# Eight pairs of heads in a recurrent block: six state steps, first blocks on three engines, one direction's streams on GpSimd, turnings between the steps, gates made once

## The chip, the cores and the metric

One Trainium2 chip, one of its cores. The metric is the device time of one execution in microseconds; everything is float32. Engines: TensorE (PE, with its weight loads PEld), VectorE (DVE), ScalarE (ACT), GpSimd (POOL), SyncE (SP), and the DMA queues.

## What is computed

Two blocks of a model run one after the other over 256 tokens of width 2048. The change touches only the second block, and in it the part called RWKV: 16 heads of 64 channels, each with two recurrences (forward and backward in time), first over 256 context tokens and then, from the state reached, over the 256 tokens of the sequence:

```python
def wkv_scan(r, w, k, v, kk, a, s0, reverse):
    def step(s, inp):
        r_t, w_t, k_t, v_t, kk_t, a_t = inp
        sa = jnp.einsum('bhij,bhj->bhi', s, -kk_t)
        s = (s * w_t[:, :, None, :] + sa[..., None] * (kk_t * a_t)[:, :, None, :]
             + v_t[..., None] * k_t[:, :, None, :])
        return s, jnp.einsum('bhij,bhj->bhi', s, r_t)
...
    y = yf + yb
    mu = jnp.mean(y, axis=-1, keepdims=True)
    var = jnp.mean(jnp.square(y - mu), axis=-1, keepdims=True)
    y = ((y - mu) * lax.rsqrt(var + GN_EPS) * ln_w + ln_b)
    y = y + jnp.sum(r * (kf + kb) * r_k, axis=-1, keepdims=True) * v
    g = jax.nn.sigmoid(gd) @ g_up
    return y.reshape(b, l, D_RWKV) * g, (sf, sb)
```

Only the outputs of the sequence are used. Its result goes, with two small mixers, through `w_out`; a feed-forward part and a norm follow.

## The kernel before, in words

The program is written out engine by engine (`sp_program`, `pool_program`, `pe_program`, `act_program`, `dve_program`); an engine does its instructions in the order of the text, and waits on semaphores by name: `need(name, j, k)` waits until pair j has counted k on that name, and `o.do(ins, S(name))` or `done(mm, name)` counts. `o.settle()` lets an engine wait for its own last instruction.

The heads are done in pairs, j = 0 to 7 (`NP2 = 8`); 128 partitions hold the two heads. Each pair has two directions, d = 0 and 1, and eight chunks of 64 tokens (`CH`): four of context, four of sequence. The programs of this stage are `pairs_pe` (from L1745), `pairs_act` (L2092), `pairs_dve` (L2423) and the loop in `pool_program` (L1474). The steps of one pair are:

- *Decays and keys.* `decays` (PE L1760, L1761) multiplies the small decay and rate weights, which GpSimd loads pair by pair (`ups`, L1460); `sigmoids` (ACT), `sums` (DVE: a scan and a subtraction), `key_sums`, `key_roots`, `key_inverse`, `key_spread`, `key_norms`, `keys` (DVE L2458), `key_mixes` and `exponentials` (ACT, three for each direction; all of pairs_act goes by the helper's line L2097).
- *Streams* (DVE L2461 to L2487, eight instructions of 128x512 or 128x256 for each direction): products of decays, keys and rates, all in SBUF. Direction 1 reads the keys backwards (`seq`). Direction 0 of the next pair is done after level 5; direction 1 in six parts between the state steps.
- *Turnings* (`by_token`, PE L1788, L1789): four for each pair, each turns two of the streams into banks 2 and 3; `token_copies` (ACT) copies both out before the next turning.
- *Scores* (PE): AX (L1801, L1803) and BR (L1813, L1817), 64x64 products of each cell, into banks 0 to 7.
- *First blocks* (`starts`, DVE L2492 to L2508): masks AX into `aT` and `xm` and makes the first level's mask `mT`; masks BR into `bT` and `rpk`; and, from the turned products (`turned_starts`, PE L1829), `xmT`.
- *Levels 1 to 5* of a triangular inversion by doubling: P (PE L1843) of `mT` and `xm`; `products` (ACT) copies; Y (PE L1856, L1858); DVE subtracts Y from `xm` and `xmT` (L2517, L2518). GpSimd makes the masks of levels 2 to 5 (L1472). Between the levels PE does head means, the gate and variances of pair j-1 and sums, decays and norms of pair j+1. DVE does, of pair j-1, `centred` (before level 1's subtractions), `variances` (before level 2's), and `normed` (before level 3's), which also multiplies by the gate in bank 7 and counts `pair_end`.
- *Right sides and solution*: `solved` (PE BV L1881, U L1888), `right_sides` (ACT: two copies within SBUF, two out of PSUM), `solutions` (ACT).
- *Steps* (PE L1900 to L1930; DVE L2548 to L2558): Z, the step matrices and the read-outs, for d = 0, then d = 1. The step matrix of a chunk is the identity minus a product.
- *States* (PE L1939, DVE `stt` of 128x64 by the helper L2436): m = 0 to 7, both directions. State 0 is zero. Streams of direction 1 and turnings 0 and 1 of the next pair stand between them, turning 2 behind them, then `outputs` (PE L1949, DVE L2572 to L2578), then turning 3 and the next scores.

The gate weights (`g_up`, 128x256 for each pair) are loaded by GpSimd in front of the masks of level 4, after `pair_end` (L1463), and the gate is computed in each pair (PE L1869). The last pair has no next one; after its level 3, DVE makes the sums of the mixed rows of pairs 0 to 6 (`mix_sums`, L2332 to L2337) for the product with `w_out`.

```python
        for j in range(NP2):
            masks(j, 2)
            masks(j, 3)
            need("pair_end", j, 0)
            gate_up(j * P, lambda ins: ...)
            masks(j, 4)
            masks(j, 5)
```

## Time and profile before

| | |
|---|---|
| median of 3 runs | 3397.76 us (3395.79 to 3398.54) |
| the profiled execution | 3396.16 us, its span 3394.3 us |
| busy, share of the span | PE 92%, PEld 82%, DVE 47%, ACT 16%, POOL 33% |
| preparation of the pairs | 1809 to 1843 us |
| the eight pairs | 1843 to 2397 us |
| PE, P of the levels (L1843) | 2560 instructions, 226 ns each |
| GpSimd, 128x512 masks (L1472) | 64 instructions, 1342 ns each |
| q8, the queue that brings instructions | 253 packets, 4.15 MB |

Times are counted from the start of the span. "Idle before" is how long an engine stood still ahead of an instruction, and the arrow names what ended it; "issue" means that nothing that the profile shows was late. Matmul records overlap, so that busy PE is not PE at its peak. PEclk is the clock that TensorE was granted, 1.00 being 2.4 GHz and 0.50 1.2 GHz.

### The profile page before, as it was taken

The page shows a single profiled execution, that of the slowest core. Times are in us where ns is not written, and L with a number is a line of the kernel's source. Part 1 is how long each engine was busy: PE and PEld are TensorE (multiplying, and loading weights), DVE is VectorE, ACT ScalarE, POOL GpSimd, SP SyncE. Part 2 cuts the span into 40 slices and gives each one's busy share as a digit, 9 for nine tenths or more (in the row PEclk, how much of TensorE's full clock was granted, in tenths as well). Part 3 has the DMA queues.
Part 4 walks back from the last instruction along what each step waited for, and adds up shares of the span by engine and source line. Part 5 has one row for each costly group of instructions (what it writes and reads, how often), then busy time and mean ns, then how long its engine had stood idle before and what let it go on. Part 6 is the DMA issues. An engine that isn't in the chain of part 4 may idle for free.

```text
span 3394.3 us, 69586 instructions
## 1 busy us (share of the span) xinstructions
PE 3112.3 (92%) x32190; PEld 2794.7 (82%) x32190; DVE 1596.5 (47%) x2384; ACT 544.6 (16%) x1022; POOL 1109.8 (33%) x621
## 2 busy tenths in 40 slices
PE   5998999998999999999896888777999999999998
PEld 4877887877878888687895777666889999999998
DVE  4745275455437610587814666666334442113111
ACT  1012112021210111100003443343010000000001
POOL 1000000000000010243671211112447797778774
PEclk8998999998999999999997999999899999999999
DMA  7955387765335643477640000000445654444443
GB/s 281 405 224 198 120 316 286 306 246 205 107 145 216 231 177 139 172 274 288 250 150 11 10 7 7 7 7 6 162 149 224 227 221 170 161 167 162 162 166 109
DMA packets 56035, 583.10 MB, mean 172 GB/s; under 512 B 7314, under 2 KB 9680, under 8 KB 10816
## 3 DMA queue, kind: packets, MB, share of 16 engines
q1 hardware_dynamic: 37808, 465.06, 36.7%
q0 software_dynamic: 17936, 113.59, 8.8%
q8 instruction: 253, 4.15, 0.5%
q14 instruction: 38, 0.31, 0.0%
HBM read 576.52 MB, written 2.10 MB: 170 GB/s over the span
## 4 chain that ended last, share of the span: by engine, by line
PE 70%; DVE 13%; DMA 9%; issue 3%; ACT 3%; POOL 2%; SPq 0%; ACTq 0%; DVEq 0%; POOLq 0%
PE PS L1675 24%; PE PS L374 14%; PE PS L672 7%; PE PS L1628 5%; DMA ring<-in_w_vec_dram 5%; DMA ring<-in_w_second_dram 2%; DVE ring L2244 2%; PE PS L417 2%; PE PS L1843 1%; DMA ring<-in_w_start_dram 1%; PE PS L371 1%; PE PS L1856 1%; PE PS L1692 1%; PE PS L1611 1%; PE PS L1888 1%
## 5 line engine op out<-in xcount | busy, mean ns | idle before, releaser
L374 PE MATMUL PS<-H,ring 128*128 128x256 f32 x2944 | 669.4, 386 | 7.0 <-ACT H L702 7.0
L374 PEld LDWEIGHTS PS<-H,ring 128*128 128x128 f32 x2944 | 562.6, 193 | 95.0 <-issue 17.6
L1675 PE MATMUL PS<-H,ring 128*128 128x128 f32 x3424 | 404.5, 276 | 1.5 <-DMA ring<-in_w_second_dram 1.5
L1675 PEld LDWEIGHTS PS<-H,ring 128*128 128x128 f32 x3424 | 394.7, 193 | 2.4 <-DMA ring<-in_w_second_dram 1.9
L2351 DVE TENSOR_TENSOR W<-W,PS 128x256 f32<-128x256 f32 x58 | 24.4, 421 | 679.8 <-ACT W L2001 679.7
L327 POOL DMA_DIRECT2D ring<-in_w_vec_dram x75 | 39.7, 530 | 923.9 <-DVE ring L888 785.7
L1675 PE MATMUL PS<-H,W 128*128 128x128 f32 x2624 | 316.6, 276 | 8.4 <-POOL W L1504 7.2
L1675 PEld LDWEIGHTS PS<-H,W 128*128 128x128 f32 x2624 | 305.0, 193 | 9.7 <-POOL W L1504 8.0
L1499 POOL TENSOR_TENSOR W<-ring 128x1024 f32<-128x1024 f32 (+1 forms) x74 | 179.7, 2429 | 265.7 <-PE PS L1675 149.2
L672 PE MATMUL PS<-H,ring 128*128 128x256 f32 x1024 | 223.5, 379 | 2.9 <-DVE H L1174 2.9
L672 PEld LDWEIGHTS PS<-H,ring 128*128 128x128 f32 x1024 | 194.2, 190 | 29.9 <-issue 3.7
L1472 POOL TENSOR_TENSOR ring<-ring,W 128x512 f32<-128x512 f32 x64 | 84.9, 1342 | 367.1 <-PE PS L1843 366.7
L888 DVE SCALAR_TENSOR_TENSOR ring<-ring,H 128x2048 f32<-128x2048 f32 x75 | 171.1, 2287 | 29.3 <-DMA ring<-in_w_vec_dram 28.6
L1504 POOL TENSOR_TENSOR W<-ring,W 128x1024 f32<-128x1024 f32 (+1 forms) x74 | 182.4, 2465 | 5.8
L1502 POOL TENSOR_TENSOR W<-W,ring 128x1024 f32<-128x1024 f32 (+1 forms) x74 | 181.6, 2455 | 0.0
L1501 POOL TENSOR_TENSOR ring<-ring 128x1024 f32<-128x1024 f32 (+1 forms) x74 | 177.4, 2398 | 5.8
L1628 PE MATMUL PS<-H,ring 128*128 128x128 f32 (+1 forms) x992 | 142.5, 306 | 9.8 <-DMA ring<-in_w_second_dram 4.9
L1628 PEld LDWEIGHTS PS<-H,ring 128*128 128x128 f32 x992 | 134.4, 199 | 16.5 <-issue 5.7
L2244 DVE SCALAR_TENSOR_TENSOR ring<-ring,W 128x2048 f32<-128x2048 f32 x48 | 127.2, 2666 | 38.5 <-DMA ring<-in_w_vec_dram 38.0
L2001 ACT ACTIVATE W<-PS 128x128 f32<-128x128 f32 (+2 forms) x61 | 18.6, 307 | 786.1 <-PE PS L1675 777.3
L1675 PE MATMUL PS<-Pj,ring 128*128 128x128 f32 x1184 | 139.8, 275 | 3.3 <-DVE H L2337 3.3
L1675 PEld LDWEIGHTS PS<-Pj,ring 128*128 128x128 f32 x1184 | 135.9, 192 | 3.5 <-issue 3.5
(500 smaller groups left out, 4990.5 us busy)
## 6 DMA issues: line engine op xcount, KB each, us to landing
ring<-in_w_second_dram SPq DMA_DIRECT2D x97, 2048.0 KB, 8.1
ring<-in_w_first_dram SPq DMA_DIRECT2D x68, 2048.0 KB, 8.3
ring<-in_w_vec_dram POOLq DMA_DIRECT2D x75, 1024.0 KB, 7.8
ring<-in_w_vec_dram SPq DMA_DIRECT2D x48, 1024.0 KB, 5.1
ring<-in_w_start_dram SPq DMA_DIRECT2D x16, 2048.0 KB, 15.7
H<-in_w_vec_dram POOLq DMA_DIRECT2D x21, 1024.0 KB, 8.1
Pj<-in_w_aside_dram SPq DMA_DIRECT2D x8, 2048.0 KB, 11.2
ring<-in_w_second_dram SPq DMA_DIRECT2D x9, 1536.0 KB, 6.6
```

The costliest lines, as they stand in the source:

```text
L374: mm = pe.matmul(PS[:, t % 2, half * T:(half + 1) * T], ring[:, t % 2, k, half * P:(half + 1) * P], hT[:, k, :], start=(k == 0), stop=(k = ...
L417: mm = pe.matmul(PS[:, t, half * T:(half + 1) * T], left, right, start=(k == 0 and half == 0), stop=(k == KC - 1), skip_group_check=True)
L672: mm = pe.matmul(PS[:, 4 + 2 * (n % 2) + half, 0:T], ring[:, t % 2, k, half * P:(half + 1) * P], hT[:, k, :], start=(k == 0), stop=(k == K ...
L888: return v.scalar_tensor_tensor(out, a, s, b, op0, op1, **kw)
L1472: S("p_mask").inc(pool.tensor_tensor(mT[d], aT[d], Ci(f"c_join{lev}").unsqueeze(1).to_broadcast([P, 8, CH]), ALU.mult))
L1499: sums.inc(pool.tensor_tensor(s_[:, 0], quarter(q, 2, nk), quarter(q, 3, nk), ALU.add))
L1501: sums.inc(pool.tensor_tensor(quarter(q, 2, nk), quarter(q, 0, nk), quarter(q, 2, nk), ALU.subtract))
L1502: sums.inc(pool.tensor_tensor(s_[:, 1], s_[:, 0], quarter(q, 0, nk), ALU.subtract))
L1504: sums.inc(pool.tensor_tensor(s_[:, 2], quarter(q, 1, nk), s_[:, 1], ALU.subtract))
L1628: mm = pe.matmul(in_regions(n % 2, wide, r), w[:, k * P:(k + 1) * P], at(m, k), start=(k == 0 and r // per not in opened), stop=(k == 7), ...
L1675: mm = pe.matmul(regions(bank2, r), w[:, k * P:(k + 1) * P], m[:, k, :], start=(first and k == 0 and r // 4 not in opened), stop=(last and ...
L2244: v.scalar_tensor_tensor(w, w, 1.0, crow2[:, 0, :], ALU.mult, ALU.mult, accum_out=mod2[:, i - 64, 0:1]).then_inc(vec_done.sem, 1)
```

## The change

- *State steps*: m = 1 to 6. Step 1 takes its state from `Z[d][:, 0]`; states 0 and 8 are no longer made (no memset).
- *First blocks*: DVE keeps `aT`, `xm`, `xmT`; GpSimd makes level 1's mask and masks `bT` and `rpk` in place (`below`); ACT copies BR out of PSUM, and does the right sides' SBUF copies there too. `xmT` of both directions is masked before the first subtraction.
- *Streams*: direction 1 goes to GpSimd (`stream_back`), in one piece, behind the masks of the pair before.
- *Turnings*: each waits bank by bank, and all four stand between the state steps 1 to 4.
- *Gates*: all weights come in one load of 1 MB on SyncE's queue, one tile before the last input tile; all eight gates are computed in the preparation and copied by ACT into `mix`.
- Pair j-1: `centred` after level 1's subtractions, variances between the two directions of level 2 on PE and DVE, the reciprocal after level 3, the rest after level 4. The mixed rows' sums go after level 4.
- Steps: the read-out subtraction before the step matrices, and a wait of PE moved behind G. `bonus` (one instruction instead of two) goes between the states. ACT does `solutions` before the second direction's exponentials.

```diff
@@ sp_program
+            if q == NIN2 - 2:
+                sp.wait_ge(vec_done.sem, vec_done.at(NL, VEC0[3] - VEC0[2]))
+                S("gate_loaded").inc(sp.dma_start(gup, A["g_up_2"][0].rearrange("(d p) c -> p d c", d=2)), 16)
@@ pool_program
         def masks(j, lev):
             for d in range(2):
-                need("p_P", j, count(lev - 1, d))
...
+                if lev == 1:
+                    need("p_aT", j, d + 1)
+                else:
+                    need("p_P", j, count(lev - 1, d))
...
+        def below(j, d):
+            need("p_BRr", j, d + 1)
+            pool.tensor_tensor(bT[d], bT[d], each8(Ci("c_supper")), ALU.mult)
+            pool.tensor_tensor(rpk[d], rpk[d], each8(Ci("c_upper")), ALU.mult)
+        def stream_back(j):
+            need("p_tm", j, 2)
+            need("p_kk", j, 1)
+            S("p_akr").inc(pool.tensor_tensor(AA[1], AA[1], seq(KK, 1), ALU.mult))
+            S("p_akr").inc(pool.tensor_tensor(TMP[1], TMP[1], seq(key(j), 1), ALU.mult))
+            need("p_bonus", j, 1)
+            need("p_akr", j, 2)
+            S("p_akr").inc(pool.tensor_tensor(BN(j).unsqueeze(1), BN(j).unsqueeze(1), TMP[1][:, 1:2, ::-1], ALU.add))
+            need("p_exp", j, 2)
+            pool.tensor_tensor(EV[1], EV[1], seq(KK, 1), ALU.mult)
+            pool.tensor_tensor(AA[1], AA[1], EN[1], ALU.mult)
+            pool.tensor_tensor(RT(j, 1).unsqueeze(1), EP[1][:, 1:2, :], seq(rec(j), 1), ALU.mult)
+            S("p_akr").inc(pool.tensor_copy(ends(j, 1), flat(EP[1])[:, CH - 1::CH]))
+            need("p_akr", j, 4)
+            S("p_strr").inc(pool.tensor_tensor(EN[1], TMP[1], EN[1], ALU.mult))
+        stream_back(0)
         for j in range(NP2):
+            masks(j, 1)
             masks(j, 2)
+            below(j, 0)
             masks(j, 3)
-            need("pair_end", j, 0)
-            gate_up(...)
+            below(j, 1)
             masks(j, 4)
             masks(j, 5)
...
+            if j < NP2 - 1:
+                stream_back(j + 1)
@@ pairs_pe
+        def gates(n):
+            for j in (2 * n, 2 * n + 1):
+                for k in range(2):
+                    mm = pe.matmul(PS[:, gate_banks[n], (j % 2) * T:(j % 2 + 1) * T], gup[:, k, j * P:(j + 1) * P], GD[:, k, :], ...)
+            done(mm, "mix_gate")
         def by_token(j, r):
...
+            for w in range(2):
+                if r:
+                    need("p_tokc", j, taken(r - 1, w))
+                elif j:
+                    need("p_step", j - 1, 2)
+                for n in range(4):
+                    mm = pe.transpose(PS[:, 2 + w, t], src[w][:, t], ident)
+                done(mm, "p_tokT")
@@ level: the variances between the directions of Y
+                if d and between:
+                    between()
@@ head_means
-            for k in range(2):
-                mm = pe.matmul(PS[:, 7, 0:T], gup[:, k * P:(k + 1) * P], GD[:, k, :], start=(k == 0), stop=(k == 1))
@@ the pair on TensorE
             steps(j)
-            for m in range(8):
+            for m in range(1, 7):
                 state(j, m)
-                if after and m in (1, 3):
-                    by_token(j + 1, m // 2)
-            if after:
-                by_token(j + 1, 2)
+                if after and m < 5:
+                    by_token(j + 1, m - 1)
             outputs(j)
             if after:
-                by_token(j + 1, 3)
                 scores(j + 1)
@@ pairs_act
+        def below(j):
+            need("p_tokc", j, 8)
+            for d in range(2):
+                f("p_act", kbv[d]..., Ktok_[d]..., ACT.Copy)
+            for d in range(2):
+                need("p_BR", j, d + 1)
+                f("p_BRr", br[d], PS[:, 4 + 2 * d:6 + 2 * d, :].rearrange(...), ACT.Copy)
...
             right_sides(j)
+            solutions(j)
             if after:
                 exponentials(j + 1, 1)
-            solutions(j)
-            if after:
                 for r in range(4):
                     token_copies(j + 1, r)
+                below(j + 1)
@@ pairs_dve
+            need("p_xt", j, 1)
+            for e in range(2):
+                o.do(v.tensor_tensor(per_head(xmT[e]), heads(2, e * T), each(Ci("c_join0")), ALU.mult))
+            o.settle()
+            for e in range(2):
+                o.do(stt(xmT[e], xmT[e], -1.0, all8(Ci("c_ident")), ALU.mult, ALU.add), S("p_x0"))
@@ the pair on VectorE
             starts(j)
+            level(j, 1)
             if before:
                 centred(j - 1)
-            level(j, 1)
-            if before:
-                variances(j - 1)
-            level(j, 2)
+            level(j, 2, (lambda: variances(j - 1)) if before else None)
             if after:
                 key_squares(j + 1)
-            if before:
-                normed(j - 1)
             level(j, 3)
             if after:
                 key_inverse(j + 1)
+            if before:
+                inverse(j - 1)
+            level(j, 4)
+            if before:
+                normed(j - 1)
...
-            for m in range(8):
+            for m in range(1, 7):
                 state(j, m)
-                if after and m < 6:
-                    stream(j + 1, 1, m)
+                if m == 1:
+                    bonus(j)
             outputs(j)
```

## Rows read from the trace of the kernel before

**Rows 1.** The page's part 4: the chain that ended last, by engine.
```profile
PE 70%; DVE 13%; DMA 9%; issue 3%; ACT 3%; POOL 2%; SPq 0%; ACTq 0%; DVEq 0%; POOLq 0%
```

**Rows 2.** Busy time by stretch: start:end, length, each engine, PEclk, DMA share, GB/s.
```profile
1809.00:1843.00 34.00, 18.56 (x64) 11.58 (x68) 12.78 (x25) 16.95 (x27) 3.17 (x5) 0.55 0.07 21
...
2047.00:2117.00 70.00, 57.24 (x1794) 50.48 (x1794) 46.30 (x96) 28.48 (x52) 12.42 (x11) 0.95 0.03 8
```

**Rows 3.** Waits of TensorE, 2047 to 2117: us in total, times, longest.
```profile
PE PS L1856 <- DVE ring L2436: 2.4, 1, 2.4
PE PS L1843 <- DVE ring L2517: 2.1, 2, 1.7
...
PE PS L1843 <- issue: 1.3, 1, 1.3
PE PS L1926 <- DVE Pj L2558: 1.3, 1, 1.3
...
PE PS L1888 <- ACT ring L2097: 0.8, 1, 0.8
```

**Rows 4.** Timeline, pair 3: start, us, engine, line, operation, idle before.
```profile
2055.93 1.58 POOL L1472 TENSOR_TENSOR ring<-ring,W 128x512 f32<-128x512 f32 x1 [0.59 <-PE PS L1843]
2057.02 1.04 DVE L2436 SCALAR_TENSOR_TENSOR ring<-ring,W 128x512 f32<-128x512 f32 x1
...
2063.10 1.03 PE L1869 MATMUL PS<-Pj,W 128*128 128x256 f32 x4
2065.79 0.41 PE L1843 MATMUL PS<-ring 64*64 64x64 f32 x7 [1.66 <-DVE ring L2517]
...
2078.34 2.50 POOL L1472 TENSOR_TENSOR ring<-ring,W 128x512 f32<-128x512 f32 x2
2078.38 0.68 DVE L2517 TENSOR_TENSOR ring<-ring,PS 128x512 f32<-128x512 f32 x1
```

**Rows 5.** Busy time by short stretch, columns as in rows 2.
```profile
2058.20:2062.10 3.90, 3.77 (x128) 3.68 (x129) 1.06 (x2) 0.02 (x1) 0.00 (x0) 0.56 0.01 4
2081.90:2084.10 2.20, 2.20 (x137) 2.13 (x133) 0.94 (x2) 0.60 (x1) 1.86 (x2) 1.00 0.03 7
1813.60:1817.40 3.80, 3.75 (x4) 1.18 (x4) 0.11 (x1) 1.17 (x1) 0.00 (x0) 0.50 0.00 0
```

**Rows 6.** Groups by shape, 1840 to 2400: busy us, mean ns, idle before.
```profile
L1843 PE MATMUL PS<-ring 64*64 64x64 f32 x2560 | 94.3, 226 | 25.1 <-DVE ring L2517 18.0 <-issue 3.3 <-POOL ring L1472 3.0
...
L1472 POOL TENSOR_TENSOR ring<-ring,W 128x512 f32<-128x512 f32 x64 | 84.9, 1342 | 367.1 <-PE PS L1843 366.7
...
L2535 DVE RECIPROCAL Pj<-Pj 128x256 f32<-128x256 f32 x7 | 12.2, 1743 | 0.0
...
L2097 ACT ACTIVATE ring<-ring 128x512 f32<-128x512 f32 x16 | 9.9, 617 | 2.7 <-PE PS L1881 2.7
...
L2487 DVE TENSOR_TENSOR W<-W 128x512 f32<-128x512 f32 x14 | 9.6, 687 | 0.2
```

**Rows 7.** Timeline of TensorE in the state steps, pair 3 and the last pair.
```profile
2105.55 0.33 PE L1939 MATMUL PS<-Pj,ring 64*64 64x64 f32 x4 [0.26 <-DVE Pj L2436]
...
2107.02 0.33 PE L1939 MATMUL PS<-Pj,ring 64*64 64x64 f32 x4
...
2112.54 0.33 PE L1788 MATMUL PS<-con,W 128*128 128x128 f32 x1
...
2391.00 0.33 PE L1939 MATMUL PS<-Pj,ring 64*64 64x64 f32 x4 [0.20 <-DVE Pj L2436]
...
2391.72 0.33 PE L1939 MATMUL PS<-Pj,ring 64*64 64x64 f32 x4 [0.20 <-DVE Pj L2436]
```

**Rows 8.** The chain that ended last, first two turnings of pair 0: start, us.
```profile
1831.27 0.47 PE PS L1788
...
1834.51 0.45 PE PS L1788
```

**Rows 9.** The same chain behind the last pair's outputs.
```profile
2396.99 8.10 DMA ring<-in_w_second_dram
```

197 lines of the change are left out of this document (91 added, 106 removed).

## The prediction

> **What bounds the kernel now.** I read the page's chain first: TensorE holds 70% of it and VectorE 13% [rows 1]. The edit touches only the eight pairs of heads of the second block, so I cut that stage into stretches that run from one pair's first score matmul to the next one's. There are nine: 34 us of preparation, and then 66, 68, 70, 70, 72, 69, 71 and 68 us. In such a pair of 70 us TensorE is busy 57.2 us, VectorE 46.3, ScalarE 28.5 and GpSimd 12.4 [rows 2]. So nothing is full. TensorE stands still for some 12 us a pair, and its work itself is stretched where the granted clock is low. The pair is one chain that goes from engine to engine and back.
>
> Who ends these idle times is in the waits of that pair [rows 3]: VectorE before the first level's second products (2.4), VectorE before the second level (most of 2.1), VectorE in the eight state steps and before the outputs' first part (1.3), ScalarE before the solving products (0.8), and "issue", where no engine is late (1.3 is the longest). Whoever shortens VectorE's list at these places shortens the pair.
>
> The timeline shows two things more. The wait of 1.66 us before the second level follows the head means and four matmul records of the gate; in it VectorE does the centring of the pair before ahead of this level's subtractions [rows 4]. And the 128 matmuls of the first level's second products take 3.8 us at a clock of 0.56, while 137 of the same kind take 2.2 us at 1.00 [rows 5]; they come right after the idle 2.4 us. The 1.66 us of idleness was followed by full clock.
>
> **The lock.** In the same group a VectorE instruction that reads two SBUF operands takes 1.04 us where its mates take 0.69: it ends 0.55 us after GpSimd's instruction ends, and that one has grown to 1.58, where two of them take 2.50 [rows 4, 6]. Beside it a VectorE instruction with one operand in PSUM takes its usual 0.68 in the middle of GpSimd's work [rows 4]. So instructions of the first sort and GpSimd's take turns. The Trainium skill (SBUF — State Buffer, "Who interferes with whom") says the same of two SBUF inputs and calls it an exclusive lock; by that rule, moving one direction's streams to GpSimd buys no parallel time where VectorE runs the other direction's streams, all of whose inputs lie in SBUF.
>
> **The change, part by part**, for one of the six pairs that have a neighbour on both sides.
>
> (1) *First blocks.* VectorE loses six of its sixteen instructions there (two level masks, four masks of the second half), 0.69 us each [rows 6]. But what TensorE waits for lies at the end: after the turned products VectorE did product, subtraction, product, subtraction, and both directions had to be ready. Now two products come first and direction 0 is released after one subtraction: one instruction less, 0.6 to 1.0 us. Against it GpSimd's first and second masks and its two masks of "below" now fall beside the VectorE subtractions with two SBUF inputs, each good for up to one GpSimd instruction, 1.3 us [rows 6]. Taken: -0.5, between +0.7 and -1.6.
>
> (2) *Between first and second level.* The four gate records (0.9 us) go, since gates are made once, and the centring moves behind the subtractions, so that the 1.66 us go as well [rows 4]: 2.6 us. ScalarE's squares wait for the centring and stand before its copies of level 2, but means end about when those copies are wanted. The rest is clock: the gap before the first level's second products shrinks by part (1); if they run at full clock that is 1.8 us [rows 5]. I take half of it, as the new gap is about as long as the 1.66 us. Taken: -3.5, between -2.0 and -4.5.
>
> (3) *Levels 2 to 4.* The normalisation (a reciprocal of 1.74 us [rows 6] and three more instructions, 3.2 us together) stood before level 3's subtractions and goes to two later places, where VectorE has time until the next products end; the variance matmul is put between the two directions; GpSimd no longer waits for the pair's end to load the gate's weights before masking level 4. TensorE's waits for these are the remainder of the 2.1 [rows 3] and GpSimd's 3.0 us over eight pairs [rows 6]. Taken: -1.1 with the variance, between -0.3 and -2.0. Late next would be the next pair's first sums on VectorE, which have the decay matmuls of TensorE as cover.
>
> (4) *Right sides.* ScalarE's two copies within SBUF (0.62 us each [rows 6]) leave the place before the solving products; one of them stood before direction 0. Of the 0.8 us waited [rows 3] 0.5 goes. Taken: -0.5, between -0.3 and -0.6. At their new place, "below", they stand behind the token copies and before the copies of the BR products; the cover is the score matmuls and level 1's first products.
>
> (5) *Steps.* The subtraction of the read-outs comes before the step matrices on VectorE (0.75 us), a memset goes, and TensorE's wait for the first Z moves behind the second G: of the 1.3 us waited [rows 3] and 0.3 before, 1.4 goes. Against it, VectorE's stream for the next pair now collides with the first two GpSimd instructions of the other direction (2.7 us), just ahead of these steps. There was about 1.5 us of slack and part (4) eats 0.5: some 0.6 comes back. Taken: -0.8, between 0 and -1.9.
>
> (6) *States and turnings.* A step with a turning between it and the next takes 1.47 us (2105.55 to 2107.02), one without 0.72 in the last pair, where VectorE has nothing else [rows 7]. Now: first step 0.7, seven steps with two turnings from 2105.55 to 2112.54, 7.0, and two more turnings of 1.1 behind: 9.9. New: four steps with a turning, 5.9, and two without, 0.8 each: 7.5. VectorE also sheds the eight stream instructions between the steps. Taken: -2.3, between -1.5 and -2.6.
> What covers it: the third turning needs GpSimd's stream. Its two first instructions start with the keys, together with VectorE's own stream; the second half (EV, AA, RT, ends, EN: three of 1.34, one of half that, 4.7 us) starts after the exponentials, which ScalarE now does behind the solution copies. By the timeline that puts its end some 2.4 us before the third turning is due. If that cover is gone, each us over 2.4 is a us on the pair.
>
> Sum for such a pair: -0.5 -3.5 -1.1 -0.5 -0.8 -2.3 = **-8.7 us**, six times: -52. Pair 0 has no (2) and (3): -4. The last pair has no turnings; its states lose two steps of 0.72, it saves 2.5 us on levels 3 and 4, because the normalisation no longer stands ahead of level 3 and the sums of the mixed rows go one level later, and gives 0.5 back there: -9 with (1), (2) and (5).
>
> *Preparation.* Now the turnings start at 1831.27 and follow each other every 3.24 us, since one waits for both copies of the other [rows 8]. New: two banks alternate, so that a turning costs about 1.6 us: 3 x 1.6 = 5 us less. But GpSimd's stream ends there near 1836 if nothing else changes, which gives some 2 of them back, and the four groups of gates, sixteen matmuls, go in: eight into TensorE's idle time before the keys, and eight behind the key norms. They cost 3.5 us for each eight at full clock, 7 at half. Against that the decay matmuls run at 0.50 now, 3.8 us [rows 5], and with the gates ahead of them TensorE is not idle before. Bounds: nothing gained at half clock; -9 at full. Taken: -5.
> The gate's weights (1 MB) move from GpSimd's queue to SyncE's, ahead of the last input tile; a load of 2 MB takes 8.1 us [rows 9], and TensorE takes longer than that for an input tile, which is the cover. Cost nothing; with the cover gone, half a load, 4 us once. *Tail*: SyncE's loads start with the last output and TensorE waits 8.1 us for them [rows 9]; this is unchanged and only comes earlier. What follows is TensorE at over 90% and moves as a whole.
>
> Sum: -52 -4 -9 -5 = -70 us. The profiled execution took 3396.16 us (span 3394.3 and 1.9 around it), 1.6 under the median 3397.76 of the three runs; so 3396 - 70 = **3326 us**.
>
> **Rivals.**
> *A, the clock comes back* (chance 0.20). With TensorE busy in more of the pair, first products and turnings run at 1.00 throughout. Then (1) and (2) reach their ends (-1.3, -4.5), (5) -1.4: about -11.5 a pair, -95 in all, 3301. For: the half-speed stretches all follow idle times that shrink. Against: the new gap before the first level's second products is no shorter than some that were followed by it.
> *B, the lock takes a share* (0.15). Each of GpSimd's 24 instructions a pair (8 now, beside its DMAs) meets VectorE's two-operand ones more often than I placed them: (1) +0.5, (2) -2.6, (5) 0, (6) -1.5, so -5 a pair, -40 in all: 3356. For: the collision in rows 4 cost each of the two 0.3 to 0.4 us. Against: most of GpSimd's masks fall beside VectorE instructions that read PSUM.
> *C, slower* (0.04): GpSimd's stream is late for the third turning. No row has GpSimd reading backwards (step -1), and five of its ten instructions do. It decides when the stream ends 2.4 + 8.7 = 11 us later than I place it. At five times the 1.34 us, these take 6.7 each: 16.7 us before the exponentials' part and 12.7 for it, 29.4 from the keys on, where I place the end at 11.6; that is 18 us, or 15 behind the slack: +6.7 a pair, +40 for the six, +11 for pair 0, -9 for the last, +10 in the preparation: 3448. VectorE's backward reads cost nothing more in its rows, so this is unlikely.
> *D, TensorE's "issue" waits fill up* (0.08): they are 3 us a pair, in dense stretches of small matmuls. If the supply of instructions is the limit there, a denser pair meets more of them, and half of the gain goes: 3361.
> *E, no change* (0.03): the six terms are all waits that something just behind also ends.
> The forecast itself has 0.50.
>
> **Numbers.** Faster: 0.50 + 0.20 + 0.15 + 0.08 = 0.93; same 0.03; slower 0.04 (0.2%, 7 us, is what a measurement of this kernel can tell from no change). The forecast's own ends, half way to the terms' ends, are 3308 and 3348; to hold eight in ten the range goes to A's value and past B's: 3298 to 3362.
>
> **What would show it.** Pairs of some 61 us instead of 70; no wait of TensorE for VectorE's subtraction before the second level; first level's second products at 1.00 in some pairs; states and turnings in 7.5 us with the outputs right behind; GpSimd busy some 25 us a pair; VectorE's streams longer than 0.69 us each beside GpSimd's. Wrong it would be if the turnings waited for GpSimd, if the level masks came late, or if the preparation grew by the gates.

## The result, and the profile of the changed kernel

The changed kernel takes **3319.44 us** in the median of four runs (3315.47 to 3320.62), the kernel before 3398.15 us in the same session (3395.79 to 3400.12): a ratio of 0.977, with an interval of 0.975 to 0.978. The forecast was 3326 us with a range from 3298 to 3362. The profiled execution took 3319.18 us (span 3317.4), against 3396.16 for the one that the sum was made on: -77.0 us where -70 was expected.

The chain of the page, by engine, in the place of [rows 1]: TensorE keeps its share.

```profile
PE 70%; DVE 14%; DMA 9%; issue 3%; POOL 2%; ACT 1%; SPq 0%; ACTq 0%; DVEq 0%; POOLq 0%
```

Busy time by stretch, columns as in [rows 2]: the preparation, pair 0, pair 3 and the last pair, cut at the first score matmul of each pair.

```profile
1805.87:1836.60 30.73, 19.04 (x90) 13.93 (x88) 14.03 (x20) 20.37 (x32) 13.26 (x13) 0.89 0.07 23
1836.60:1898.06 61.46, 51.33 (x1764) 45.69 (x1765) 38.67 (x67) 31.89 (x56) 28.80 (x24) 0.97 0.03 7
2018.94:2078.18 59.24, 51.52 (x1783) 45.30 (x1780) 43.34 (x76) 30.74 (x54) 28.84 (x24) 1.00 0.03 7
2258.35:2316.30 57.95, 46.04 (x1731) 41.99 (x1727) 37.27 (x66) 13.56 (x25) 18.55 (x14) 0.91 0.02 4
```

Pair 3 went from 70.3 to 59.2 us. TensorE is busy 5.7 us less in it and idle 5 us less; GpSimd went from 12.4 to 28.8 us. The waits of TensorE in this pair, in the place of [rows 3]:

```profile
PE PS L1906 <- DVE ring L2496: 2.6, 2, 2.0
PE PS L1972 <- DVE Pj L2599: 1.0, 1, 1.0
PE PS L1947 <- issue: 1.0, 1, 1.0
PE PS L1891 <- issue: 0.9, 1, 0.9
...
PE PS L1934 <- ACT ring L2145: 0.3, 1, 0.3
```

The first row, the wait before the first level's second products (L1906), is as long as before (2.4 then). The wait for VectorE's subtraction before the second level (2.1 us at the line of the levels' first products before) is gone; the issue wait of 0.9 at that line (L1891) stands in the first level, at 2025.8. The solving products (L1934) wait 0.3 for ScalarE, not 0.8.

The same place in the timeline, in the place of [rows 4]: VectorE's two subtractions with both operands in SBUF, and GpSimd beside them.

```profile
2028.20 1.27 POOL L1482 TENSOR_TENSOR ring<-ring,W 128x512 f32<-128x512 f32 x1 [0.60 <-PE PS L1891]
2028.56 3.14 DVE L2496 SCALAR_TENSOR_TENSOR ring<-ring,W 128x512 f32<-128x512 f32 x2
2029.42 1.73 POOL L1487 TENSOR_TENSOR ring<-ring,W 128x512 f32<-128x512 f32 x1
2031.10 1.73 POOL L1488 TENSOR_TENSOR ring<-ring,W 128x512 f32<-128x512 f32 x1
```

Two subtractions take 3.14 us, and each of GpSimd's masks of BR beside them 1.73 where the mask of level 2 (L1482) takes 1.27. The mask of level 2 had started first, before the subtraction. The same happens in the streams of the next pair: GpSimd's first two instructions take 1.70 and 1.72, and VectorE's second 1.76 instead of 0.69.

```profile
2059.94 0.69 DVE L2525 TENSOR_TENSOR W<-W,Pj 128x512 f32<-128x512 f32 x1
2060.06 1.70 POOL L1494 TENSOR_TENSOR W<-W,Pj 128x512 f32<-128x512 f32 x1 [6.18 <-DVE Pj L2518]
2060.55 1.76 DVE L2526 TENSOR_TENSOR W<-W,Pj 128x512 f32<-128x512 f32 x1
2061.72 1.72 POOL L1495 TENSOR_TENSOR W<-W,Pj 128x512 f32<-128x512 f32 x1
...
2066.66 1.27 POOL L1500 TENSOR_TENSOR W<-W,Pj 128x512 f32<-128x512 f32 x1 [1.89 <-ACT W L2145]
2070.07 1.27 POOL L1505 TENSOR_TENSOR W<-W 128x512 f32<-128x512 f32 x1
```

L1500 reads one operand backwards and still takes 1.27. The stream ends at 2071.34; the third turning, which needs it, starts at 2073.49. The steps, in the place of [rows 7]:

```profile
2071.61 0.33 PE L1986 MATMUL PS<-Pj,ring 64*64 64x64 f32 x4
...
2073.08 0.33 PE L1986 MATMUL PS<-Pj,ring 64*64 64x64 f32 x4
...
2076.61 0.33 PE L1986 MATMUL PS<-Pj,ring 64*64 64x64 f32 x4 [0.27 <-DVE Pj L2496]
...
2077.42 0.68 PE L1996 MATMUL PS<-Pj 64*64 64x64 f32 x16 [0.29 <-DVE Pj L2496]
```

A step with a turning takes 1.47 us as before, and from the first step (2070.21) to the outputs it is 7.2 us.

**Phases.** To compare kernels I took from the trace when the first record of each kind of product starts, and averaged over the six middle pairs. The columns: from the first scores to the first level's second products; from there to the first products of level 2; levels 2 to 4; level 5 and the right sides up to the solving products; from these to the first step; from the first step to the next pair's scores; the sum; then pair 0, the last pair, and the preparation, from the end of the transform's products to the first scores. Each kernel's phases come from its one profiled execution. The time before this stage, in which nothing was edited in any run, lasted 1798.6 to 1808.7 us in the profiles of the changed kernel and its variants, so that a difference of some us between two totals need not lie in the pairs.

| kernel | scores, level 1 | to level 2 | levels 2-4 | level 5, right sides | solving, steps' products | states, turnings, outputs | pair | pair 0 | last | prep. |
|---|---|---|---|---|---|---|---|---|---|---|
| before | 11.6 | 7.3 | 21.2 | 8.4 | 10.3 | 11.3 | 70.0 | 66.2 | 67.7 | 35.0 |
| changed | 11.5 | 4.4 | 18.0 | 7.9 | 10.2 | 8.0 | 60.0 | 61.5 | 57.8 | 30.7 |
| forecast of the difference | -0.5 | -3.5 | -1.1 | -0.5 | -0.8 | -2.3 | -8.7 | -4 | -9 | -5 |
| measured difference | -0.1 | -2.9 | -3.2 | -0.5 | -0.1 | -3.2 | -10.0 | -4.7 | -9.9 | -4.3 |

What TensorE does in these phases, us a pair over the same six pairs (waits over 0.15 us, from the trace):

| | scores, level 1 | to level 2 | levels 2-4 | level 5, right sides | solving, steps' products | states, turnings, outputs | pair |
|---|---|---|---|---|---|---|---|
| waits for an engine, before | 2.4 | 1.7 | 0.5 | 1.1 | 1.4 | 2.1 | 9.2 |
| the same, changed | 2.1 | 0.4 | 0.0 | 0.6 | 1.2 | 0.6 | 4.8 |
| issue waits, before | 1.3 | 0.4 | 2.0 | 0.0 | 0.4 | 0.0 | 4.1 |
| the same, changed | 1.9 | 0.0 | 0.4 | 0.0 | 0.6 | 0.0 | 3.0 |
| busy, before | 7.8 | 5.3 | 18.6 | 7.3 | 8.5 | 9.2 | 56.6 |
| the same, changed | 7.6 | 4.0 | 17.6 | 7.3 | 8.3 | 7.4 | 52.2 |

So the 10.0 us are 4.4 of waits for other engines, 4.4 of TensorE's own busy time and 1.1 of issue waits. In the busy time there is the work that was taken away, and up to 1.4 us of clock: the granted clock over these pairs rose from 0.968 to 0.986.

### The profile page after: what moved, and what is told of

It reads as the page before. It is cut to its first block, busy times and chain, and to the rows that moved or that the text cites. A ratio compares the mean times of both kernels' runs of the same rounds, so it can differ in the third digit from the quotient of the medians.

```text
span 3317.4 us, 69293 instructions
## 1 busy us (share of the span) xinstructions
PE 3078.1 (93%) x32062; PEld 2768.7 (83%) x32062; DVE 1578.4 (48%) x2216; ACT 564.4 (17%) x1042; POOL 1234.7 (37%) x725
## 3 DMA queue, kind: packets, MB, share of 16 engines
q8 instruction: 252, 4.13, 0.5%
## 4 chain that ended last, share of the span: by engine, by line
PE 70%; DVE 14%; DMA 9%; issue 3%; POOL 2%; ACT 1%; SPq 0%; ACTq 0%; DVEq 0%; POOLq 0%
PE PS L1712 23%; PE PS L374 15%; PE PS L672 7%; PE PS L1665 5%; DMA ring<-in_w_vec_dram 4%; DMA ring<-in_w_second_dram 2%; PE PS L1891 2%; DVE ring L2304 2%; PE PS L417 2%; DMA ring<-in_w_start_dram 1%; PE PS L371 1%; PE PS L1908 1%; PE PS L1906 1%; PE PS L1837 1%; PE PS L1729 1%
## 5 line engine op out<-in xcount | busy, mean ns | idle before, releaser
L374 PEld LDWEIGHTS PS<-H,ring 128*128 128x128 f32 x2944 | 562.1, 193 | 94.9 <-issue 17.6
L672 PEld LDWEIGHTS PS<-H,ring 128*128 128x128 f32 x1024 | 194.2, 190 | 29.9 <-issue 3.7
L1482 POOL TENSOR_TENSOR ring<-ring,W 128x512 f32<-128x512 f32 x80 | 101.0, 1276 | 159.2 <-DVE ring L2543 82.5
L2049 ACT ACTIVATE W<-PS 128x128 f32<-128x128 f32 (+2 forms) x61 | 18.6, 307 | 789.5 <-PE PS L1712 780.5
L2145 ACT ACTIVATE ring<-PS 128x512 f32<-128x512 f32 (+2 forms) x232 | 121.6, 568 | 162.1 <-PE PS L1891 56.6
## 6 DMA issues: line engine op xcount, KB each, us to landing
Pj<-in_w_aside_dram SPq DMA_DIRECT2D x8, 2048.0 KB, 11.3
```

The lines of the kernel that those rows point to most:

```text
L374: mm = pe.matmul(PS[:, t % 2, half * T:(half + 1) * T], ring[:, t % 2, k, half * P:(half + 1) * P], hT[:, k, :], start=(k == 0), stop=(k = ...
L672: mm = pe.matmul(PS[:, 4 + 2 * (n % 2) + half, 0:T], ring[:, t % 2, k, half * P:(half + 1) * P], hT[:, k, :], start=(k == 0), stop=(k == K ...
L1482: S("p_mask").inc(pool.tensor_tensor(mT[d], aT[d], each8(Ci(f"c_join{lev}")), ALU.mult))
L2145: S(name).inc(act.activation(out_, in_, fn, **kw))
```

## The experiments

**Centring first.** The one order on VectorE that the change turned round is turned back.

```diff
-            level(j, 1)
             if before:
                 centred(j - 1)
+            level(j, 1)
             level(j, 2, (lambda: variances(j - 1)) if before else None)
```

> The changed kernel with one thing undone: VectorE does the centring of the pair before ahead of level 1's subtractions again, not behind them. TensorE's order stays. By step (2) of the prediction this wait is worth 1.66 us in each of the seven pairs that have one before them, and some clock may go with it: 1.7 to 2.6 us a pair, 12 to 18 in all, 3331 to 3337 us, and TensorE's idle time of about 1.7 us for VectorE behind the head means is back. Rival (GpSimd's masks for level 2 end there just behind, so that the order on VectorE is worth little): under 0.5 us a pair, 3319 to 3323. Clock theory (the order matters only because the idle time costs clock): the phase grows by no more than 1 us where the granted clock stays, and by 2 or more where it falls.

Measured: 3344.40 us, ratio 0.984 (0.982 to 0.987), 25 us above the changed kernel where 12 to 18 were expected. A pair takes 63.2 us instead of 60.0. The phase to level 2 grows by 1.8 us, and levels 2 to 4 by 1.2. The waits of TensorE over the six middle pairs of this run:

```profile
PE PS L1906 <- DVE ring L2496: 14.9, 11, 2.1
PE PS L1891 <- DVE ring L2559: 10.0, 6, 1.7
PE PS L1891 <- issue: 7.4, 6, 1.5
```

The second row is the wait of 1.66 us that was foretold: 10.0 over six, and it fills the 1.8 us. The rest is no wait for VectorE: all issue waits of these pairs sum to 22.1 us instead of 17.8, 0.7 a pair, and TensorE is busy 0.6 us more a pair at a clock of 0.98 instead of 0.99 (316.8 against 313.0 over six). TensorE's program is the same to the last instruction, so the issue waits are worth a look of their own.

**Turnings late.**

```diff
-                if after and m < 5:
-                    by_token(j + 1, m - 1)
+                if after and m in (2, 4):
+                    by_token(j + 1, m // 2 - 1)
+            if after:
+                by_token(j + 1, 2)
             outputs(j)
             if after:
+                by_token(j + 1, 3)
```

> The changed kernel with the four turnings back at their old places relative to the steps: the first two behind the second and fourth of the six steps, the third behind the last step, the fourth behind the outputs. Six steps are kept. By step (6): two steps with a turning (1.47 each), four without (0.72 to 0.8) and two turnings alone (1.1 each) make 8.1 us where the changed kernel has 7.3 to 7.5: +0.6 to 0.8 us in each of seven pairs, +4 to +6, 3323 to 3325. Rival (GpSimd's stream is just in time for the third turning, and what the denser order wins is given to waits): -0.5 to +0.3 a pair, 3316 to 3321.

Measured: 3325.17 us, ratio 0.978 (0.977 to 0.980); a pair takes 61.3 us. Steps, turnings and outputs went from 8.0 to 8.7 us: +0.7, as priced. The other 0.6 lies in the phase to level 2 at a lower clock (0.97 over these pairs against 0.99).

**Eight steps.** Steps 1 and 6 are done twice.

```diff
-            for m in range(1, 7):
-                state(j, m)
-                if after and m < 5:
-                    by_token(j + 1, m - 1)
+            for i, m in enumerate((1, 1, 2, 3, 4, 5, 6, 6)):
+                state(j, m, i + 1)
+                if after and i < 4:
+                    by_token(j + 1, i)
```

> The changed kernel with eight state steps a pair again: the first and the sixth are done twice, with the same values, and the four turnings stay behind the first four. By step (6) each extra step without a turning costs 0.72 to 0.8 us: +1.5 us a pair over eight pairs, +12, 3331 us. Rival (the two steps were hidden: TensorE has the next pair's turnings to do and VectorE's chain is not what ends last): +0 to +3, 3319 to 3322.

Measured: 3344.05 us, ratio 0.983 (0.980 to 0.986), again 25 us above, where 12 were expected; the four runs lie far apart (3326.62 to 3350.35). The phase of the steps grew from 8.0 to 9.7, +1.7 for two steps: the price of step (6) holds. But the pair grew by 3.3, and in it the issue waits by 1.3 (25.4 us over six pairs against 17.8); TensorE's lower clock, 0.97, is in the rest.

**Masks held.** GpSimd waits for the end of VectorE's subtractions.

```diff
             masks(j, 2)
+            need("p_x0", j, 2)
             below(j, 0)
```

> The changed kernel with one wait more on GpSimd: its two masks of direction 0 of what lies below (of BR) wait until VectorE's last subtraction of the first blocks is over. Nothing is moved on another engine. Lock theory (VectorE's instruction with two SBUF operands and GpSimd's take turns, and the subtraction of 3.14 us with the record at 2028.56 is 1.3 us of work and the rest GpSimd's masks): the longest of these subtractions falls to 2 us or less, TensorE's waits for it (2 x 1.3 us) lose 1.2 to 2 us a pair, 10 to 14 us in all: 3305 to 3310. Rival (a subtraction with these operands is simply slow there, or GpSimd's level 2 mask alone does it): under 0.5 us a pair, 3316 to 3321. Against both: if GpSimd's masks of level 3 come late because of the hold, up to 1 us a pair the other way.

Measured: 3322.23 us, ratio 0.977 (0.975 to 0.980), where 3305 to 3310 was expected. The profiled execution, 3313.53 us, was the fastest of four (the slowest 3327.75), so that the total shows no gain and the phases have to. Pair 3 of that run:

```profile
2030.52 1.27 POOL L1482 TENSOR_TENSOR ring<-ring,W 128x512 f32<-128x512 f32 x1 [0.60 <-PE PS L1892]
2030.88 2.06 DVE L2497 SCALAR_TENSOR_TENSOR ring<-ring,W 128x512 f32<-128x512 f32 x2
2033.02 1.27 POOL L1487 TENSOR_TENSOR ring<-ring,W 128x512 f32<-128x512 f32 x1 [1.23 <-DVE ring L2497]
```

The two subtractions fell from 3.14 to 2.06 us, and the mask of BR from 1.73 to 1.27 though nothing in either instruction changed. So they do take turns. The chain gained 0.8 us a pair in this profile, less than the 1.2 to 2 expected: the phase to level 2 has 3.09 us in the pairs at full clock against 3.84. The first subtraction still meets the mask of level 2, and the phase up to the first level's second products stays, with the same wait for VectorE in it, 2.05 us a pair.

**Stream held.**

```diff
             need("p_tm", j, 2)
-            need("p_kk", j, 1)
+            need("p_streams", j, 1)
```

> The changed kernel with GpSimd's streams of the next pair held until VectorE's own stream is over (before, both started with the keys). Lock theory: VectorE's eight stream instructions fall from up to 1.76 us to 0.69 each, its stream ends 1.5 to 2 us earlier, and the phase from the solving products to the outputs' first part, 9.23 us, loses 1 to 1.8. GpSimd's stream ends 1 us later than now, so the third turning, which has some 2 us of slack now and less then, waits 0 to 1 us. Sum -0.5 to -1.5 us a pair, 3309 to 3316 us. Rival (the phase is set by TensorE's own products, not by VectorE's stream): the phase stays at 9.2, the turning waits, 3319 to 3325. So far two runs of each kernel of the same text differ by up to 5 us in the preparation by its clock alone, so the phases of the pairs decide.

Measured: 3328.89 us, ratio 0.981 (0.978 to 0.984), where 3309 to 3316 was expected; the profiled execution, 3318.43 us, was the fastest of the four. A pair takes 60.0 us in it, as without the hold. VectorE in pair 3 of this run:

```profile
2061.60 0.69 DVE L2525 TENSOR_TENSOR W<-W,Pj 128x512 f32<-128x512 f32 x1
2062.21 0.68 DVE L2526 TENSOR_TENSOR W<-W,Pj 128x512 f32<-128x512 f32 x1
...
2064.88 0.69 DVE L2537 TENSOR_TENSOR W<-W 128x512 f32<-128x512 f32 x1
2066.43 0.76 DVE L2595 TENSOR_TENSOR ring<-PS,H 128x256 f32<-128x256 f32 x2 [0.86 <-PE PS L1947]
```

VectorE's stream takes 4.0 us (2061.60 to 2065.57) where it took 6.5: the collisions cost VectorE 2.5 us. But then it waits 0.86 us for TensorE's products, and the phase lost only 0.3 us. The expectation for the lock's duration was right and the one for its place on the path wrong: most of it hits time that VectorE had to spare. TensorE's waits for VectorE in this phase fell by 0.6 us a pair (1.2 to 0.6), but its issue waits there rose by 0.5 (0.6 to 1.1), so that half of what was won went to those.

**Gate again.** Two more products of 256 columns ahead of the head means.

```diff
+                for k in range(2):
+                    pe.matmul(PS[:, 6, 0:T], ones64, YF, start=(k == 0), stop=(k == 1))
             pe.matmul(PS[:, 6, 0:T], ones64, YF, start=True, stop=True)
```

> The changed kernel with two more products of 256 columns ahead of the head means in each pair, of the size of the gate's that the change took away (their values are not used). By step (2) they cost 0.9 us a pair, +6 us over seven: 3325. Rival (hidden: TensorE stands there until VectorE's subtraction of level 1 is over anyway): +0.3 us a pair or less, 3319 to 3321. Clock theory: filling the gap with work keeps the clock up, so the half speed time in the middle pairs falls and the phase does not grow: 3317 to 3320.

Measured: 3340.86 us, ratio 0.983 (0.980 to 0.986), where 3325 was expected; the profiled execution took 3329.58 us, the fastest of the four. The phase to level 2 grew by 0.8, as priced. The pair grew by 2.4, and 1.4 of it stands in level 3, two levels behind the added products, where TensorE now waits in each of the six pairs with no engine late:

```profile
2045.96 0.27 PE L1906 MATMUL PS<-ring 64*64 64x64 f32 x2 [1.18 <-issue]
```

**Gates behind.** The first two groups of gates come behind the key norms, with the others.

```diff
-        gates(0)
-        gates(1)
         key_sums(0)
...
         key_norms(0)
+        gates(0)
+        gates(1)
         gates(2)
```

> The changed kernel with the first two groups of gates (eight matmuls) behind the key norms in the preparation, with the other two, instead of ahead of the key sums, so that TensorE stands idle before the decay matmuls as it did in the kernel before. Clock theory (prediction's preparation part: with the gates ahead TensorE is not idle before): the two pairs of decay matmuls go from 1.96 us back to 3.75 each, the preparation grows by 2 to 4 us; the pairs stay. Rival (the gates only fill idle time, the clock does not matter): the gates cost TensorE's time behind the key norms, where it waits for the streams, +0 to +1. In the time of the whole kernel both lie near what can be told.

Measured: 3325.36 us, ratio 0.979 (0.977 to 0.982). The decay matmuls took 3.75 us each and the preparation 33.7 us. That looked like the clock theory, until the other profiles were laid beside it: of the runs with the gates ahead most had slow decay matmuls too, and then a preparation of 35.1 us, longer than this one. So a control was run.

**The changed kernel again**, unaltered, in a later session.

> The changed kernel itself, unaltered, as a control on the chip of the next two: what differs between two runs of one text. From the eight profiles so far: the first decay matmuls of the preparation took 1.95 us in three runs and 3.5 to 3.75 in five, with the same edit there in all but one, and the preparation 30.7 or 35.1 us. If that is chance of the run and not of the kernel, this profile shows one of these two values, and the median lies between 3317 and 3326 us. In the pairs every phase but the first two and the ones beside an issue wait should repeat to 0.1 us.

Measured: 3322.61 us in the median of five (3319.34 to 3330.14), ratio 0.979 (0.977 to 0.981). The pairs repeat (60.1 us), the preparation does not: 35.1 us. The first decay matmuls in the first run of the changed kernel:

```profile
1811.66 1.10 PE L1800 MATMUL PS<-Pj,W 96*128 96x512 f32 x2 [1.49 <-DVE H L2501]
1812.60 1.02 PE L1801 MATMUL PS<-Pj,W 96*128 96x512 f32 x2
```

and in the control:

```profile
1807.35 2.03 PE L1800 MATMUL PS<-Pj,W 96*128 96x512 f32 x2 [1.51 <-DVE H L2501]
1809.18 1.91 PE L1801 MATMUL PS<-Pj,W 96*128 96x512 f32 x2
```

The same idle time stands before them, 1.49 and 1.51 us, and so do the same gates; once the granted clock is 1.00 (2.4 GHz), once 0.50 (1.2 GHz). Of the twelve profiles of this study with the gates ahead, three had the short form (1.95) and nine the long one (3.2 to 3.75).

**Streams on VectorE.** On GpSimd the call of the second direction's streams is gone; the first hunk is VectorE's, the second TensorE's:

```diff
                 state(j, m)
+                if after and m < 5:
+                    stream_back(j + 1, m - 1)
                 if m == 1:
                     bonus(j)
...
                 if after and m < 5:
-                    by_token(j + 1, m - 1)
+                    by_token(j + 1, m - 1) if m < 3 else None
+                if after and m > 4:
+                    by_token(j + 1, m - 3)
```

> The changed kernel with the other direction's streams on VectorE again, two of their instructions behind each of the first four of the six state steps, and the third and fourth turnings, which need them, behind the fifth and sixth step. GpSimd keeps the masks. It tells what the move to GpSimd is worth by itself. Lock theory (two engines that take turns win no time): VectorE's own stream runs at 0.69 an instruction again, the phase from the solving products to the outputs' first part loses 1 to 1.8 us as in the run with the held stream, and the steps gain 1 to 2: -0.5 to +1 us a pair, 3316 to 3326. Rival (the move took real work off the chain): steps and turnings grow by 2 us or more and nothing comes back: 3333 or more.

Measured: 3332.45 us, ratio 0.981 (0.979 to 0.984); a pair takes 62.1 us. The steps grew by 1.6 us and the phase before them lost only 0.1; 0.8 more stand in the phase to level 2, at a clock of 0.96 over the pairs. So the move to GpSimd, with the places of the third and fourth turning that it allows, is worth 1.5 to 2 us a pair, lock or no lock; the two were not separated. In the preparation it is the other way: 27.7 us against 30.7 at the same clock.

**Two moves.** The held masks, and in the preparation alone the first pair's second streams on VectorE behind its own.

```diff
             masks(j, 2)
+            need("p_x0", j, 2)
             below(j, 0)
...
-        stream_back(0)
...
         stream(0)
+        stream_back(0)
```

> The changed kernel with GpSimd's masks of direction 0 held until the subtractions of the first blocks are over (as in the run with the masks held), and with the first pair's second streams, in the preparation alone, on VectorE behind its own, since the run with all streams on VectorE had a preparation of 27.7 us where the changed kernel has 30.7. Lock theory: both only take away collisions, so they add up: -3 us in the preparation, -0.75 to -1 us a pair, 9 to 11 us below the control on the same chip. Rival (what VectorE wins the chain loses to issue waits or to clock): under 4 us below the control.

Measured: **3314.43 us** in the median of four (3308.83 to 3315.43), ratio 0.975 (0.974 to 0.977), beside the control's 3322.61 and 0.979 (0.977 to 0.981): 8.2 us below it, where 9 to 11 were expected, and the best kernel of this study. The preparation took 29.9 us with the slow decay matmuls, 5.2 below the control's; a pair 59.3, 0.9 below.

**Normalisation early.**

```diff
+            if before:
+                inverse(j - 1)
+                normed(j - 1)
             level(j, 3)
             if after:
                 key_inverse(j + 1)
-            if before:
-                inverse(j - 1)
             level(j, 4)
-            if before:
-                normed(j - 1)
```

> The changed kernel with the normalisation's reciprocal and its three further VectorE instructions (3.2 us together) back ahead of level 3's subtractions. By step (3) of the prediction this costs the wait of TensorE before level 3 or 4 again: +0.3 to +2.0 us a pair, +1.1 taken, so +2 to +14 us over seven pairs, with the phase of level 2 to 3 or of 3 to 4 growing by it. Rival (there is room: VectorE waits 2.6 us for the products of level 3 in the changed kernel): of 3.2 us 2.6 are covered, +0.6 a pair or less. Issue theory (what moves here is the waits for instructions, which fall on fixed matmul counts): the phase moves by no more than 0.3 and the matmul counts between issue waits stay multiples of 127.

Measured: 3322.84 us, ratio 0.978 (0.977 to 0.980), the control's time. Levels 2 to 4 take 18.2 us against 18.0. A pair is 1.1 us longer, but in phases that the edit does not touch, at a clock of 0.97. The move of the normalisation is worth 0.2 us at most.

**Shifted code.** The kernel of the two moves with 32 tiny products more, once, in the preparation.

```diff
+        for n in range(32):
+            pe.matmul(PS[:, 6, 0:2], ident, ones64[:, 0:2], start=True, stop=True)
         for r in range(4):
             by_token(0, r)
```

> The kernel of the two moves with 32 tiny products more on TensorE (64 records, two columns each), once, in the idle time of the preparation behind the gates. Nothing in any pair changes; only the count of instructions ahead of them does. Supply theory (TensorE's issue waits come where a new block of its instructions is due, each 127 matmul records, whatever stands there): the issue waits move by 64 records to other lines in every pair, off the BR and first level products at the pair's start, distances stay multiples of 127, and their sum over the six middle pairs, 17.0 us in the run of the two moves, changes by more than 2 us, up or down, and the pairs' time with it. Rival (the issue waits belong to these places in the program, such as many small products in a row): same lines, same sum within 1 us, same time.

Measured: **3341.16 us**, ratio 0.982 (0.979 to 0.985), 27 us above the kernel of the two moves. The tiny products were dearer than thought, and not hidden. The first 36 records ran at a clock of 1.00, 0.11 us each; then the granted clock fell to 0.50 in the midst of them, with TensorE never idle, and the next 29 took 0.21 each:

```profile
1825.47 10.08 PE L2012 MATMUL PS<-con 128*128 128x2 f32 x64
```

so that the preparation grew by 9.0 us (29.9 to 38.9). But the six middle pairs, in which no instruction changed, went from 355.6 to 383.1 us. (The totals differ by less than the sum of the two: in this profile the time before the stage was 5.8 us shorter and the time behind the last outputs 5.9.) The busy time of these six pairs in both, columns as above, first the two moves:

```profile
1899.41:2254.97 355.56, 311.21 (x10654) 274.87 (x10650) 253.49 (x451) 184.09 (x324) 166.56 (x142) 0.99 0.03 7
```

```profile
1900.91:2284.04 383.13, 322.62 (x10652) 285.06 (x10649) 254.08 (x451) 184.20 (x324) 166.53 (x142) 0.96 0.02 6
```

and the waits of TensorE by the name of issue, first the two moves, with a sum of 17.2 us:

```profile
PE PS L1891 <- issue: 5.8, 6, 1.2
...
PE PS L1947 <- issue: 3.6, 3, 1.2
PE PS L1861 <- issue: 3.1, 3, 1.0
...
PE PS L1865 <- issue: 2.4, 3, 0.9
...
```

then the shifted code, with a sum of 29.2:

```profile
PE PS L1877 <- issue: 7.7, 6, 1.5
PE PS L1861 <- issue: 4.4, 3, 1.8
PE PS L1865 <- issue: 4.2, 3, 1.5
...
PE PS L1908 <- issue: 3.4, 4, 1.2
...
PE PS L1851 <- issue: 3.2, 3, 1.3
PE PS L1849 <- issue: 3.1, 3, 1.1
```

The waits before the first level's first products (L1891) are gone, and those in the G products (L1947) too; new ones stand at the scores (L1849, L1851), the turned starts (L1877) and in the second products of the levels (L1906, L1908). The distances between them, counted in matmul records of the trace, stayed near multiples of 127 (128, 127, 506, 253, 762, and so again in each of the first pairs). That and the sum are as the supply theory had them. One point is not: the BR products (L1861, L1865) keep a wait, since with a grid of 127 and a shift of 64 the next crossing moves in there. The waits themselves make 12.0 of the 27.6 us; TensorE's busy time grew by 11.4 at the lower clock, 0.96 against 0.99; the rest is longer waits for VectorE. Whether the waits bring the lower clock was not tried by itself, and the clock moves without them: the run with the gates behind has the changed kernel's pairs to the instruction, a clock of 0.97 over them and 365.3 us for the six instead of 360.3. So the 12.0 us are the shift's, and the 11.4 only in part for sure.

## Why the prediction was right, and where not

The total and its place were right: the eight pairs are 74.6 us shorter (554.2 to 479.6 from the first scores to the last outputs), and most of it is what was named, waits of TensorE for VectorE's list and work taken from TensorE. The terms were less good than their sum. Three of the six for a pair promised 1.7 us too much and two gave 3.0 too little; that this nearly cancels, and that 1.1 of the 10.0 us were issue waits which no term contained, is luck.

- **(1) First blocks**, -0.5 foretold, -0.1 measured. The waits for VectorE fell by 0.4 and TensorE's busy time by 0.2, but the issue waits in this phase rose by 0.6 (1.3 to 1.9), which the term did not have. The collisions were priced for the wrong place: GpSimd's masks of BR lengthen the two subtractions to 3.14 us, 2.06 without them, but the wait before the first level's second products is 2.05 us a pair in both cases. What they cost, 0.8 us, falls in the next phase. Whether the mask of level 2, which meets the first subtraction in every run, keeps this wait was not tried.
- **(2) Between level 1 and 2**, -3.5 foretold, -2.9 measured. The two prices hold one by one: 1.8 us for the centring's place, 0.8 us for the gate's products. In pair 3 the first level's second products ran at full clock, and so in two of the other five. This is the best founded step.
- **(3) Levels 2 to 4**, -1.1 foretold with bounds of -0.3 and -2.0, **-3.2 measured: the step that failed**, by mechanism too. Of the 3.2 us 1.6 are issue waits (2.0 to 0.4 a pair; in four of the six pairs before, one of 1.0 to 1.2 us stood in the second products of level 3, and none there after), a cost that the term had at nothing. The waits for VectorE and GpSimd that it did price were 0.5 and went whole, and about 1.0 is TensorE's busy time, up to 0.5 of it clock. The move of the normalisation, for which I gave most of the term, is worth 0.2 us. With the centring turned back 1.2 us come back in these levels, 0.5 of them issue waits. The variance between the two directions and GpSimd's wait before level 4 were not tried alone.
- **(4) Right sides**, -0.5 foretold, -0.5 measured (8.4 to 7.9, the same in every kernel of the study).
- **(5) Steps**, -0.8 foretold, -0.1 measured. The collisions took 2.5 us of VectorE's stream where I had put 2.7, so that their size was right. What I missed is how little is won without them: the phase is 9.9 us then instead of 10.2, since TensorE's own products and its issue waits come next.
- **(6) States and turnings**, -2.3 foretold, -3.2 measured. Prices hold: +1.7 for two steps, +0.7 for the old places. The 7.5 us came out as 7.2. I had left out that the fourth turning stood behind the outputs: from the outputs to the next scores it went from 2.45 to 0.76 us, -1.7, of which I had counted one turning of 1.1.
- **Preparation**, -5 foretold, -4.3 in the profiled execution and +0.1 in the control. The turnings came as foretold: from the first one to the first scores it is 6.5 us in both, 11.5 before. What stands against them was missed: beside GpSimd's stream VectorE's own takes 9.1 us (1820.94 to 1830.07 in the control) where it took 4.0, so that the first turning starts 5 us later. I had given 2 for GpSimd. The 4.4 us between the two executions are the clock: the decay matmuls run at 1.00 in one and at 0.50 in the other, and the gates ahead of them don't prevent it.
- **Pair 0 and the last**, -4 and -9 foretold, -4.7 and -9.9 measured.

The rivals. *A*: the clock of the six middle pairs rose from 0.97 to 0.99, which is 1.4 us a pair at the most; three of the six pairs still have a half-speed stretch, and the further 2.8 us a pair did not come. (By its own terms this rival makes -11.1 a pair, not -11.5.) *B*: the lock is there, and of GpSimd's and VectorE's durations it was the largest new thing in the trace, but its share of the path was small: 0.8 us a pair behind the first blocks, 0.3 at the streams, and some 5 us once in the preparation. The sentence of the Trainium skill (SBUF — State Buffer, "Who interferes with whom"), that such a pair of instructions holds an exclusive lock, is borne out by the change of both durations when one is held. What I drew from it, that the move to GpSimd buys no parallel time, was wrong for the pairs: it bought 1.5 to 2 us a pair, since only the first three of GpSimd's eight instructions (there are eight, not ten) meet VectorE's stream, and the others fall beside instructions that read PSUM. In the preparation, where both streams run alone, it held. *C*: backward reads cost nothing (1.27 us), with 2.1 us left before the third turning. *D*: the issue waits did not fill up, they fell from 24.5 to 17.8 us over the six middle pairs (4.1 a pair before, where I had put 3), 1.1 us of the 10.0 a pair. That is no merit of the change: the shifted code has 29.2 with pairs in which nothing but the count ahead of them differs. As an estimate, with the issue waits of before the changed kernel would be at 3319 + 7 = 3326 us, and with the shifted code's 27.6 us at 3347. The range of the forecast covers both, but not because I had thought of it: where the grid of the instruction stream falls was in none of its terms.

## What to carry to other kernels

Price an edit at the place where its wait ends: here the order of two groups of instructions on VectorE was worth 1.8 us a pair, and the move of four others 0.2. A collision of GpSimd and VectorE counts only where the slowed instruction is awaited; look there first, and hold GpSimd back there rather than undo the move. In dense stretches of small matmuls the count of instructions ahead of them is a variable of its own: before a difference under 1% is put down to an edit, compare the issue waits of stretches that the edit does not touch.

## What the runs showed of the hardware

**Issue waits fall on a grid of instructions.** They are up to 2.0 us long (before; 1.4 in the changed kernel, 1.8 in the shifted code) and stand at distances that are near multiples of 127 matmul records of TensorE. The page's row of DMA queues has a queue for instructions:

```profile
q8 instruction: 252, 4.13, 0.5%
```

4.13 MB in 252 packets is 16.4 KB each, and in the 59.24 us of pair 3 this queue moves 14 packets while TensorE has 1783 matmul records: 127 to a packet. The Trainium skill (Runtime: NRT & Kernel Launch, "Instruction fetch mechanics") says that an engine's instructions are fetched in blocks of 16 KiB, 256 instructions, and that crossing a block is mostly hidden. The size agrees (a record of a matmul and one of its weight load make two instructions, 254 in all); that it is hidden holds at most crossings only: of 84 in the six middle pairs (14 each) 20 show a wait of over 0.25 us in the changed kernel and 26 in the shifted code, nearly all among 64x64 matmuls that stand close, and of 0.7 to 1.5 us mostly. The packets fit the waits in time as well: the 16 longest of the 20 end 1.2 to 1.6 us after a packet of this queue has landed, and so do 23 of the 26. Moving the grid by 64 records, with no change in the pairs, went with 4.6 us a pair, 2.0 of them these waits and 1.9 busy time at the lower clock.

**The clock after the same idle time.** After 1.5 us of idleness the same decay matmuls ran at 1.00 in one run and at 0.50 in another of the same kernel, 4.4 us of preparation apart. What stood just before the gap, the gates at 1.00, was the same too.

**The lock stretches both sides.** Two VectorE subtractions took 3.14, 2.06 with one GpSimd instruction beside them instead of three; GpSimd's took 1.73 beside them and 1.27 alone. Copies within SBUF, with a single operand, are stretched as well; in the control's preparation, beside GpSimd's stream:

```profile
1823.34 1.25 DVE L2528 COPY Pj<-W 128x256 f32<-128x256 f32 x1
1827.65 1.22 DVE L2534 COPY H<-W 128x8 f32<-128x8 f32 x1
```

and in the run of the two moves, with GpSimd idle:

```profile
1829.48 0.29 DVE L2528 COPY Pj<-W 128x256 f32<-128x256 f32 x1
1831.23 0.17 DVE L2534 COPY H<-W 128x8 f32<-128x8 f32 x1
```
